# One packed table word per tile in a two-layer mixture-of-experts trunk

## The reference

```python
def grouped_moe(h, router_w, router_bias, w_gate, w_up, w_down):
    t = h.reshape(-1, d)
    scores = jax.nn.sigmoid(t @ router_w)
    ...   # one group of 4 experts per token, the top 2 inside it
    gates = ...   # the two chosen scores, normalised, zero elsewhere
    a = silu(einsum('td,edf->tef', t, w_gate)) * einsum('td,edf->tef', t, w_up)
    y = einsum('tef,efd->td', a * gates[:, :, None], w_down)
```

## Time and profile before

| | us |
|---|---|
| median of 3 runs | 1817.98 |
| lowest and highest | 1814.69, 1820.83 |
| span of the profiled execution, first to last instruction | 1812.5 |
| tiles of layer 0, first to last gate product | 567.9 to 874 |
| tiles of layer 1 | 1438.5 to 1758 |

### The profile page before, as it was taken

The page is one execution under the profiler, slowest core; times in us unless marked ns, Lnnn a source line. Parts: engine busy times, 40 slices in busy tenths (PEclk is TensorE's granted clock), DMA queues, the critical chain, the costliest instruction groups (busy, mean ns, idle before and its releaser), DMA issues.

```text
span 1812.5 us, 17004 instructions
## 1 busy us (share of the span) xinstructions
PE 1533.8 (85%) x5355; PEld 850.0 (47%) x5356; DVE 856.0 (47%) x1548; ACT 258.0 (14%) x507; POOL 150.2 (8%) x267
## 2 busy tenths in 40 slices
PE   3799999989955999999359989987997489999980
PEld 2684544458843444444134334432886344444430
DVE  3554686644243332232353999966224422223326
ACT  2210000001121111111130000005112011111112
POOL 2000000000000111011310000000001011011104
PEclk9999999999986999999769989998999599999995
DMA  9574066560143666794532335442004567556727
GB/s 334 160 279 154 25 217 210 169 202 1 47 181 121 231 221 219 268 327 155 189 128 65 99 91 131 105 107 81 1 1 163 186 221 281 200 189 238 281 80 280
DMA packets 196430, 300.79 MB, mean 166 GB/s; under 512 B 12021, under 2 KB 153425, under 8 KB 196384
## 3 DMA queue, kind: packets, MB, share of 16 engines
q1 hardware_dynamic: 169952, 205.94, 36.1%
q0 software_dynamic: 17696, 62.24, 9.5%
q10 hardware_dynamic: 8736, 31.99, 4.5%
HBM read 248.51 MB, written 51.53 MB: 166 GB/s over the span
## 4 chain that ended last, share of the span: by engine, by line
PE 63%; DMA 16%; DVE 13%; issue 2%; ACT 2%; SPq 1%; POOL 1%; DVEq 0%; POOLq 0%; ACTq 0%
PE bank L886 19%; PE bank L964 15%; PE bank L1005 13%; DMA W<-in_moe_w_down 12%; PE bank L1020 6%; DVE W L1183 3%; DVE R L1604 3%; PE bank L996 2%; DVE R L1161 2%; PE bank L1109 1%; DMA W<-in_ada_w 1%; PE bank L869 1%; DVE X L1161 1%; PE bank L1142 1%; PE bank L903 1%
## 5 line engine op out<-in xcount | busy, mean ns | idle before, releaser
L886 PE MATMUL bank<-HTR,W 128*128 128x512 f32 x1024 | 451.4, 599 | 7.2 <-DVE R L1591 7.2
L1005 PE MATMUL bank<-W,R 128*128 (+1 forms) x816 | 369.5, 606 | 31.0 <-DMA W<-in_moe_w_down 14.2
L886 PEld LDWEIGHTS bank<-HTR,W 128*128 128x128 f32 x1024 | 193.9, 192 | 244.6 <-issue 244.0
L1161 DVE TENSOR_TENSOR R<-bank,R 128x256 f32<-128x256 f32 (+1 forms) x91 | 49.3, 542 | 540.6 <-ACT R L686 339.0
L1005 PEld LDWEIGHTS bank<-W,R 128*128 128x128 f32 x816 | 153.0, 192 | 217.8 <-issue 213.8
L964 PE MATMUL bank<-W,R 128*128 128x256 f32 x1024 | 231.1, 385 | 9.0 <-ACT R L786 7.8
L964 PEld LDWEIGHTS bank<-W,R 128*128 128x128 f32 x1024 | 194.6, 193 | 38.6 <-ACT R L786 8.7
L1604 DVE SCALAR_TENSOR_TENSOR R<-R,PT 128x998 f32<-128x998 f32 (+21 forms) x152 | 195.1, 1284 | 5.4
L1020 PE MATMUL bank<-W,R 128*128 x408 | 187.1, 602 | 3.8 <-DVE R L1412 3.8
L1183 DVE SCALAR_TENSOR_TENSOR W<-W,CAB 128x256 f32<-128x256 f32 x308 | 149.3, 485 | 11.0
L1020 PEld LDWEIGHTS bank<-W,R 128*128 128x128 f32 x408 | 74.7, 193 | 79.7 <-issue 79.7
(11 more groups left out here) (191 smaller groups left out, 945.6 us busy)
## 6 DMA issues: line engine op xcount, KB each, us to landing
W<-in_ada_w SPq DMA_DIRECT2D x48, 1024.0 KB, 11.6
W<-in_moe_w_gate SPq DMA_DIRECT2D x32, 1024.0 KB, 7.4
W<-in_moe_w_up SPq DMA_DIRECT2D x32, 1024.0 KB, 11.0
W<-in_moe_w_down SPq DMA_DIRECT2D x32, 1024.0 KB, 12.9
y_scratch<-R ACTq DMA_DIRECT2D x51, 512.0 KB, 7.5
W<-glu_scratch SPq DMA_DIRECT2D x48, 258.0 KB, 4.6
W<-in_conf_w SPq DMA_DIRECT2D x12, 1024.0 KB, 8.8
W<-in_hyb_w_in SPq DMA_DIRECT2D x10, 1024.0 KB, 12.9
```

The costliest lines, as they stand in the source:

```text
L886: ins = pe.matmul(dst[:], lhs(k), rhs(k), start=(k == 0), stop=(k == kc - 1))
L1005: ins = pe.matmul(M[0][:], XT[:, k, :], W[:, bass.ds(at + k * 2 * FE, 2 * FE)], start=(k == 0), stop=(k == KC - 1))
L1161: return dve.tensor_tensor(o, a, b, op)
```

## The change

RT shrinks to two parts. Part 0 stays. Part 1 holds one word per tile: the lowest three groups of three bits are the number of experts loaded into buffers 0, 1 and 2, and the bits above are the buffer's number (512 for each). TensorE reads this word at the head of the loop and once more for `down`, and works out thresholds and offset with shifts, masks and multiplications in registers. The first tile's `gate_up` is written out with constants.

```diff
-        RT = sb("RT", [1, 5 * MAXT], I32)
+        RT = sb("RT", [1, 2 * MAXT], I32)
...
-        RTF = HTR[0:1, 2, 0:5 * MAXT]
+        RTF = HTR[0:1, 2, 0:2 * MAXT]
...
-                def gate_up(t, at, thr):
+                def word_of(t):
+
+                    return pe.value_load(RT[0:1, bass.ds(t + MAXT, 1)], min_val=0, max_val=512 * NEB - 1)
+
+                def buffer_at(word):
+
+                    return nc.s_assert_within((word >> 9) * EXP, 0, (NEB - 1) * EXP,
+                                              skip_runtime_bounds_check_because="a tile's buffer is below NEB")
+
+                def gate_up(t, word):
                     pe.wait_ge(xt_a[l], t + 1)
                     pe.wait_ge(xt_d[l], t + 1)
                     for b in range(NEB):
-                        pe.wait_ge(e_in[l][b], thr[b])
+                        pe.wait_ge(e_in[l][b], ((word >> (3 * b)) & 7) * 48)
+                    at = buffer_at(word)
...
-                def expert_at(t):
-                    return pe.value_load(RT[0:1, bass.ds(t + MAXT * 4, 1)], min_val=0,
-                                         max_val=(NEB - 1) * EXP)
+                def first_gate_up():
+
+                    pe.wait_ge(xt_a[l], 1)
+                    pe.wait_ge(xt_d[l], 1)
+                    pe.wait_ge(e_in[l][0], 48)
+                    for k in range(KC):
+                        ins = pe.matmul(M[0][:], XT[:, k, :], W[:, k * 2 * FE:(k + 1) * 2 * FE],
+                                        start=(k == 0), stop=(k == KC - 1))
+                    ins.then_inc(gu[l], 1)
 
                 transpose_tile(16)
-
-                gate_up(0, 0, [48, 0, 0])
+                first_gate_up()
                 transpose_tile(32)
                 transpose_hidden(0)
 
                 with pe.Fori(1, nt) as t:
-                    thr = [pe.value_load(RT[0:1, bass.ds(t + MAXT * (1 + b), 1)], min_val=0, max_val=48 * NE)
-                           for b in range(NEB)]
-                    gate_up(t, expert_at(t), thr)
+                    gate_up(t, word_of(t))
                     transpose_tile(t * 16 + 32)
-                    down(t - 1, expert_at(t - 1))
+                    down(t - 1, buffer_at(word_of(t - 1)))
                     transpose_hidden(t)
-                down(nt - 1, expert_at(nt - 1))
+                down(nt - 1, buffer_at(word_of(nt - 1)))
...
-                    link(dve.tensor_scalar(RTF[:, (1 + b) * MAXT:(2 + b) * MAXT],
-                                           ROWT[:, (2 + b) * MAXT:(3 + b) * MAXT], 48.0, None, ALU.mult))
-
-                bf = ROWT[:, 5 * MAXT:6 * MAXT]
-                link(dve.scalar_tensor_tensor(out=bf, in0=ROWT[:, 2 * MAXT:3 * MAXT],
-                                              scalar=-float(NEB), in1=ex, op0=ALU.mult, op1=ALU.add))
-                link(dve.tensor_scalar(RTF[:, 4 * MAXT:5 * MAXT], bf, float(NEB), float(EXP),
-                                       ALU.add, ALU.mult))
+
+                def loaded(b):
+                    return ROWT[:, (2 + b) * MAXT:(3 + b) * MAXT]
+                word, rest = RTF[:, MAXT:2 * MAXT], ROWT[:, 5 * MAXT:6 * MAXT]
+                link(dve.tensor_scalar(rest, loaded(0), 1.0 - 512.0 * NEB, 512.0 * NEB, ALU.mult, ALU.add))
+                link(dve.scalar_tensor_tensor(out=word, in0=ex, scalar=8.0, in1=loaded(2),
+                                              op0=ALU.mult, op1=ALU.add))
+                link(dve.scalar_tensor_tensor(out=word, in0=word, scalar=8.0, in1=loaded(1),
+                                              op0=ALU.mult, op1=ALU.add))
+                link(dve.scalar_tensor_tensor(out=word, in0=word, scalar=8.0, in1=rest,
+                                              op0=ALU.mult, op1=ALU.add))
                 link(dve.tensor_copy(RT[:], RTF))
```

## The result

The changed kernel takes 1796.51 us in the median of 4 runs (1794.08 to 1798.32), the kernel before beside it 1819.4. The ratio is 0.988 with a 95% interval of 0.9862 to 0.9897: 22.9 us faster. Measured again on chip 2, with 13 executions of the kernel before, the same pair stood at 0.9895 (0.9878 to 0.9911), 20.3 us. The forecast was 1793.5 with 24.4 us of gain, so it was near in the total. Not all of its terms were. One execution of a later kernel, 1822.84 us with the split alone, was in a slower state of the chip (mean granted clock 0.899, the others 0.929 to 0.937) and is left out.

A forecast was written before the change was run, and what follows sets the result against it. TensorE was taken as held between tiles by table loads that its sequencer starts late. 39 tiles by 0.56 us plus 2.6 us in first tiles gave 24.4 us, from 1817.98 to 1793.5 us, range 1788 to 1802.

The forecast's parts named there:

- The short gaps: Before each ordinary tile's first gate product, TensorE loses 0.56 us to sequencer steps; removing them makes the period 11.39, from 11.95.
- The first tiles: First loop tile of each layer, where the array is empty: 1.4 us won in layer 0, 1.2 in layer 1.
- What is added: TensorE's register arithmetic on the word: 0.5 us a tile as four fused instructions, bounds 0 to 1.25 us, hidden in ordinary tiles.
- VectorE: Table writing in `route`: some 0.2 us less work, hidden behind a 1.47 us wait for the product of L987; gain zero.
- The tiles tied to weights: Four loop tiles wait for expert transfers; distances over two tiles stay fixed, so 8 tiles gain nothing.
- rival (3): Weight transfers crowd with shorter tiles; four waits and two close ones give back 4 to 6 us: 1798 to 1799; chance 0.08.
- The sum and its base: Whole kernel: 39 tiles by 0.56 us plus 2.6 make 24.4 us; span 1812.5 becomes 1788.1, median 1793.5.
- the 5.5 us between span and median: Whole kernel: the median 1817.98 lies 5.5 us above the profiled span 1812.5, a distance taken as unchanged.
- (2): TensorE's table loads don't bind, so only noise or the first tiles change: 1815 to 1818; chance 0.04.
- the lead that the prediction set beside it: TensorE's 64-deep queue lets engine instructions queue while control instructions execute, so loads would be covered already and gain nothing.
- (1): TensorE's arithmetic on the word is dearer than its nearest row; halfway, gain some 12 us, 1806; chance 0.09.
- (4): On TensorE's sequencer every derived value gets its own range check; 39 tiles lose 14 us: 1832; chance 0.03.

The follow-up runs named there:

- the split alone: Packed kernel with gate and up weights issued once the buffer's last gate products are done, down under its own semaphore: 1777.78 us, ratio 0.9777.
- the pair without weight waits: Kernel before and packed kernel, each with part of the weight transfers of experts 3 to 15 left out: 1804.42 us and 1773.69 us.

## Why the prediction was right, and where it wasn't

**The short gaps.** Right: 0.56 us a tile from the sequencer's steps, period 11.39 forecast and 11.40 measured. The first tiles gained 1.38 and 1.20 us where 1.4 and 1.2 were said. In layer 0 that fit is partly luck: the wait itself fell by 1.19 (3.27 to 2.08), and the other 0.18 came from the first tile's products, 10.15 us before and 9.97 after, which the change doesn't touch. That the cause is the place behind the wait, and not the count of the loads, is shown by four loads ahead of it (0.9889) and by one extra load that costs nothing.

**What is added.** Inside its bounds, above the value taken. I took 0.5 us for four fused instructions. It is eight single ones at 0.1 us and 0.05 us more in the first address, about 0.85. My reason for one fused instruction per value was wrong: only the address fused. In ordinary tiles it did not matter, since 0.9 us was to spare; with two loads more it would have. In the first tiles it is paid: the weight load starts 1.13 us behind the evictions in layer 0 (579.16 to 580.29), where I had 0.85.

**VectorE.** Right. It waits 1.70 us for L987 behind the shorter table, 1.47 in the earlier trace rows.

**The tiles tied to weights.** The mechanism holds, its size was off, and a term was missing. I said that 8 tiles gain nothing and that their distances stay. The third part is still issued 12.7 to 13.0 us behind the start of the tile two before, the slow clock aside, where I had 12.75. But only one of the four distances stayed (26.81 to 26.92); the other three grew by 0.96 to 2.98 us, 6.5 in all, and a slow clock behind the second wait cost 1.7 more. Together that is some 8 us in the profiled pair.

Two steps failed. The larger is the clock, which was in no step of the sum: the products behind three of the waits take 8.82, 8.71 and 8.66 us in place of 7.03, which is 5.1 of the 8 us, and two of these three lie inside a distance that grew. The smaller, some 3 us, is that I carried each transfer through with the length seen in one execution: from issue to landing the third parts take 14.2, 13.1, 13.2 and 11.8 us now, 12.0, 12.3, 13.8 and 12.5 before, and the tile starts 0.2 to 0.8 us behind the landing, not 0.2 to 0.3.

Neither is shown to be an effect of the change. The second profile of the kernel before has its waits at 15.2 us instead of 8.3 and a slow clock behind three of them. The four distances add up to 102.8 and 113.9 us in the two profiles of before, 109.2 and 112.0 in the two of after. Two against two don't decide my rival (3), that the transfers crowd when tiles are shorter.

**The sum and its base.** In spans I forecast 24.4 us less and got 20.2. Of the difference, about 8 us are the weight stretches just named, and 3.6 came back from parts that the change doesn't touch (the start of the tiles 1.1 earlier, the part between the layers 2.0 shorter, the tail 0.5), by which single executions differ. I had also taken the 5.5 us between span and median as fixed. The profiled execution after took 1794.08 with a span of 1792.3, 1.8 below it; 1812.5 was thus most likely a short execution of the kernel before, not one with 5.5 us around it. In every execution for which both are on record the span lies 1.7 to 1.9 us below the time. With the typical execution as a base the handing back is 8 to 10 us, as the pair without weight waits says, where I had 4.5 (28.9 less 24.4). The 3 to 6 us beyond it are of the size that rival (3) named (4 to 6); whether they come from the clock or from the transfers isn't shown. That the total came out within 1.5 us is thus partly luck: the gain without waits for weights was 1.8 us larger than said (30.7 for 28.9), which covered a part of what was handed back.

**The rivals.** (2), that the loads don't bind, is refuted by both profiles, and with it the lead that the prediction set beside it: with `transpose_hidden` at the loop's end the counter starts within 0.1 us of the end of VectorE's product in every tile looked at, with one or two loads more as well. (1) was true in its premise, some 0.85 us of arithmetic for 0.5, and had 1.5 us of room. (4) never came near, since no derived value got a check of its own.

**Open.** Why the transfers of single-tile experts take 13 us in one execution and 15 to 17 in others (ahead of tile 16, from the issue of the first part to the landing of the third) wasn't tried, nor what decides whether the clock falls. The idle time alone doesn't: the first loop tile of layer 0 in the kernel before starts after 3.27 us of idle in both profiles, and its 16 products take 7.13 us in one and 8.82 in the other; with one load more, 2.38 us of idle was enough, in the packed kernel without waits for weights even 1.92, and 3.20 was not in the first profile of before.

## What to carry to other kernels

Look at what the sequencer does between a wait that is met late and the next product: register loads placed behind such a wait are paid in full once the array's remaining work runs out, and cost nothing ahead of it. Moving them is worth as much as packing them. The price is nothing up to a limit and what lies beyond it after that, not an even share: in an ordinary tile one load more was free here, the second cost 0.35 us. And take a second profile of the same kernel before a sum relies on the length of its waits for transfers or on the clock behind them; then ask for a buffer's data when its last reader is done, part by part, before looking for bandwidth.

## What the runs showed of the hardware

A load of one integer by TensorE's sequencer takes 0.30 us and its whole bundle 0.66 to 0.75; a plain register operation 36 ns, one per 0.1 us. After gaps of 1.9 to 5.4 us the array often, not always, came back at the lower clock (0.50 to 0.66 granted over the next 4 us in the stretches read), and its 16 products took 8.5 to 10.2 us in place of 7.0 or 7.1. A gap of a few microseconds cost 1.4 to 3.1 us beyond itself in these cases and nothing in others, up to a gap of 3.27 us in the first profile of before.
